# A two-layer trunk on one core: scan inputs on row quarters of TensorE, the angle products on ScalarE, the copies of q between the sines, three products of zeros at the begin in place of five

## The reference

```python
for l in range(DEPTH):                       # 2 layers
    h = rms_norm(x, norm1_g[l])
    u, q, k, v, g_ssm, g_attn = jnp.split(h @ w_in[l], splits, axis=-1)
    y_ssm = s5_branch(u, ...)                # below
    q = apply_rope(rms_norm(q, q_norm_g[l]), cos, sin)
    k = apply_rope(rms_norm(k, k_norm_g[l]), cos, sin)
    y_attn = moba_attention(q, k, v) @ w_attn[l]     # causal, one block of 256
    x = x + (sigmoid(g_ssm) * y_ssm + sigmoid(g_attn) * y_attn) @ w_out[l]
    x = x + hier_moe(rms_norm(x, norm2_g[l]), ...)   # 2 of 32 experts of width 512

# s5_branch: abar = exp(lam * dt) is complex, per group and state
bu = einsum('bsgh,gph->bsgp', u, bbar)       # re and im
s[t] = abar * s[t-1] + bu[t]                 # the scan over 256 tokens
y = re(einsum('bsgp,ghp->bsgh', s, c)) + d_skip * u
z = gelu(y);  val, gate = split(z @ w_glu);  return val * sigmoid(gate)
```

## Time and profile before

| | us |
|---|---|
| median of 3 runs | 1342.66 (1339.72 to 1344.41) |
| the profiled execution, its time | 1342.33 |
| its span, first to last instruction | 1340.4 |
| TensorE products busy | 1166.9 (87% of the span) |
| VectorE / ScalarE / GpSimd busy | 427.3 / 179.9 / 170.8 |
| DMA, mean over the span | 345 GB/s |
| mean granted clock of TensorE | 0.935 |

### The profile page before, as it was taken

How to read it: one execution, slowest core, us unless ns; L and a number is a source line. 1 busy time by engine, 2 the same in 40 slices (tenths; PEclk the granted TensorE clock), 3 DMA queues, 4 the chain that set the end, 5 groups by cost and what they waited for, 6 DMA issues and landing times.

```text
span 1340.4 us, 18306 instructions
## 1 busy us (share of the span) xinstructions
PE 1166.9 (87%) x7416; PEld 520.6 (39%) x7417; DVE 427.3 (32%) x863; ACT 179.9 (13%) x375; POOL 170.8 (13%) x186
## 2 busy tenths in 40 slices
PE   9999999999866887787799999999988876877677
PEld 6445546433321332233264455464333322332232
DVE  5789742411100110011087987232111101110011
ACT  1412412200000000000025124040000000000000
POOL 1757400000000000000035672000000000000000
PEclk9999999999988887898899999999998879888888
DMA  7533566999999999999973236869999999999997
GB/s 264 187 126 126 209 277 272 374 426 425 428 428 426 429 429 428 427 429 427 408 236 131 120 127 252 353 258 379 428 427 426 429 429 428 427 429 429 429 422 292
DMA packets 66520, 462.32 MB, mean 345 GB/s; under 512 B 20792, under 2 KB 21024, under 8 KB 40352
## 3 DMA queue, kind: packets, MB, share of 16 engines
q1 hardware_dynamic: 65680, 461.44, 83.4%
q10 hardware_dynamic: 784, 0.09, 0.0%
HBM read 460.47 MB, written 1.05 MB: 344 GB/s over the span
## 4 chain that ended last, share of the span: by engine, by line
PE 50%; DMA 38%; DVE 5%; SPq 4%; issue 2%; ACT 1%; DVEq 0%; ACTq 0%
DMA pool_all<-in_w_gate_up_dram 34%; PE ps L1077 16%; PE ps L825 8%; PE ps L859 4%; PE ps L1091 3%; SPq L522 3%; PE ps L884 3%; DMA pool_all<-in_w_down_dram 3%; PE ps L709 2%; PE ps L840 2%; PE ps L1036 2%; PE ps L728 1%; PE ps L743 1%; PE ps L1013 1%; PE ps L893 1%
## 5 line engine op out<-in xcount | busy, mean ns | idle before, releaser
L1077 PE MATMUL ps<-pool_all,xs 128*32 128x512 f32 (+1 forms) x2816 | 370.5, 687 | 134.7 <-DMA pool_all<-in_w_gate_up_dram 122.5
L1077 PEld LDWEIGHTS ps<-pool_all,xs 128*32 128x32 f32 x2816 | 97.8, 124 | 401.4 <-issue 400.2
L1869 DVE SCALAR_TENSOR_TENSOR rope<-rope,ps 128x512 f32<-128x512 f32 x22 | 15.1, 688 | 520.8 <-ACT rope L1412 520.8
L1091 PE MATMUL ps<-pool_all 128*32 128x512 f32 (+1 forms) x1408 | 159.3, 605 | 20.3 <-DMA pool_all<-in_w_down_dram 14.1
L825 PE MATMUL ps<-pool_all,hT 128*128 128x512 f32 x256 | 114.3, 598 | 0.0
L1412 ACT ACTIVATE rope<-ps 128x512 f32<-128x512 f32 x22 | 13.1, 597 | 640.6 <-PE ps L1077 640.6
L1091 PEld LDWEIGHTS ps<-pool_all 128*32 128x32 f32 x1408 | 46.0, 111 | 119.1 <-issue 117.7
L2134 POOL TENSOR_TENSOR pool_all<-pool_all 128x512 f32<-128x512 f32 x64 | 79.5, 1275 | 26.7 <-DVE pool_all L1647 21.2
L1036 PE MATMUL ps<-xs,pool_all 128*128 128x512 f32 x176 | 81.4, 605 | 0.0
L1013 PEld LDWEIGHTS ps<-pool_all,hT 128*128 128x128 f32 x640 | 73.0, 192 | 16.8 <-issue 16.8
L1013 PE MATMUL ps<-pool_all,hT 128*128 128x128 f32 x640 | 76.8, 278 | 0.0
(11 more groups left out here) (261 smaller groups left out, 1031.7 us busy)
## 6 DMA issues: line engine op xcount, KB each, us to landing
pool_all<-in_w_gate_up_dram SPq DMA_DIRECT2D x108, 2048.0 KB, 29.0
pool_all<-in_w_down_dram SPq DMA_DIRECT2D x58, 2048.0 KB, 26.8
pool_all<-in_w_in_dram SPq DMA_DIRECT2D x14, 2048.0 KB, 13.0
pool_all<-in_w_gate_up_dram SPq DMA_DIRECT2D x22, 1024.0 KB, 15.8
pool_all<-in_w_gate_up_dram SPq DMA_DIRECT2D x30, 512.0 KB, 7.4
pool_all<-in_w_glu_dram SPq DMA_DIRECT2D x4, 2048.0 KB, 11.1
pool_all<-in_w_out_dram SPq DMA_DIRECT2D x4, 2048.0 KB, 11.9
pool_all<-in_w_down_dram SPq DMA_DIRECT2D x6, 1024.0 KB, 19.1
```

Of the source, the lines that this page charges most:

```text
L1077: mm = pe.matmul(ps[r, half], xT[:, k // 4, k % 4, r], lane_cols(n, TRIO * h, k % 4, half), start=(k == 0), stop=(k == KC - 1), skip_group ...
L1091: mm = pe.matmul(ps[r, 2 + half], ffT[:, c, r], lane_cols(n, 2 * TRIO, c, half), start=(c == 0), stop=(c == 3), skip_group_check=True)
```

## The change

Five edits. (1) `scan_input` uses products of 32 rows (row quarters) in place of 64: the four tiles of a quad take the four quarters of the rows and write one bank each, 4 to 7; steps with even k use the left half of each bank, odd k the right half. Before, step k used only two banks, and halves of the rows. (2) Since all steps now share the four banks, step k >= 1 waits for `taken` (VectorE has done its four multiplications of step k - 1) in place of `scanned` (its scans of step k - 2), step 0 waits for `v_raw` (ScalarE has copied v), and the first glu product waits for the last scan. (3) ScalarE makes the products of step number and turns, 32 copies with a scale, of 129 columns, per layer; the low part goes to `sinT`, where the sines come later. (4) ScalarE's `heads_out(0)` stands between the sines of the first and of the second half. (5) `WARM` is 3.

```diff
-WARM = 5
+WARM = 3
+    taken = signal("taken", 8)
...
                 if k == 0:
                     pe.wait_ge(b_ready, at(b_ready, l, 4))
-                if k == 1:
                     pe.wait_ge(v_raw, at(v_raw, l, 2))
-                if k >= 2:
-                    pe.wait_ge(scanned, at(scanned, l, k - 1))
+                if k >= 1:
+                    pe.wait_ge(taken, at(taken, l, k))
                 for part in range(2):
-                    for j in (0, 2, 1, 3):
-                        r = slice(64 * (j // 2), 64 * (j // 2) + 64)
-                        mm = pe.matmul(ps[:, 4 + 2 * (k % 2) + j // 2, (2 * part + j % 2) * P:(2 * part + j % 2 + 1) * P],
+                    for j in range(4):
+                        r = slice(32 * j, 32 * j + 32)
+                        c = SEQ * (k % 2) + P * part
+                        mm = pe.matmul(ps[:, 4 + j, c:c + P],
                                        b_lhs[r, part, j % 2, q], uT[r, q, half * HALF:(half + 1) * HALF],
                                        start=True, stop=True)
...
                     if u == 0:
-                        pe.wait_ge(scanned, at(scanned, l, 7))
+                        pe.wait_ge(scanned, at(scanned, l, 8))
...
+        def setup_steps(h):
+            for turns, dst in ((turns_hi, turn_a[:, h]), (turns_lo, sinT[:, 8 * h:8 * h + 8])):
+                for i in range(8):
+                    act.activation(dst[:, i], const("step"), ACT.Copy, scale=turns[:, 8 * h + i:8 * h + i + 1]).then_inc(stepped, 1)
...
             setup_one(l)
-            for h in range(2):
-                setup_sines(l, h)
+            setup_steps(0)
+            setup_steps(1)
+            setup_sines(l, 0)
...
             heads_out(0)
+            setup_sines(l, 1)
             heads_std(0)
...
-            ve.tensor_tensor(a, step, wide(turns_hi[:, tiles], 2, [8, TW]), ALU.mult).then_inc(dve_layer, 1)
-            ve.wait_ge(dve_layer, S.next())
+            ve.wait_ge(stepped, at(stepped, l, TILES * (h + 1)))
             ve.tensor_scalar(b, a, ROUND, ROUND, ALU.add, ALU.subtract).then_inc(dve_layer, 1)
             ve.wait_ge(dve_layer, S.next())
             ve.tensor_tensor(a, a, b, ALU.subtract).then_inc(dve_layer, 1)
             ve.wait_ge(dve_layer, S.next())
-            ve.tensor_tensor(b, step, wide(turns_lo[:, tiles], 2, [8, TW]), ALU.mult).then_inc(dve_layer, 1)
-            ve.wait_ge(dve_layer, S.next())
-            ve.tensor_tensor(a, a, b, ALU.add).then_inc(dve_layer, 1)
+            ve.tensor_tensor(a, a, sinT[:, tiles], ALU.add).then_inc(dve_layer, 1)
...
-                for o, x, table in ((0, re, cs), (1, im, sn), (2, im, cs), (3, re, sn)):
-                    ve.tensor_tensor(out4[o], x, table, ALU.mult).then_inc(dve_layer, 1)
+                for o, x, table in ((0, re, cs), (1, im, sn), (2, im, cs)):
+                    ve.tensor_tensor(pre[:, o], x, table, ALU.mult).then_inc(dve_layer, 1)
                     L.add()
+                ve.tensor_tensor(pre[:, 3], re, sn, ALU.mult).then_inc(taken, 1)
```

More of the change, by code:

```diff
@@ L373, in trunk @@
     turn_ready, one_ready, turns_ready, tables_ready = signal("turn_ready"), signal("one_ready", 2), signal("turns_ready", 2), signal("tables_ready")
-    sin_ready, half_ready = signal("sin_ready", 2), signal("half_ready", 2)
+    stepped, half_ready = signal("stepped_or_sine", 2 * TILES + 2), signal("half_ready", 2)
     f_ready, expanded = signal("f_ready"), signal("expanded", 4)
@@ L384, in trunk @@
     first_rows, first_xT = signal("first_rows"), signal("first_xT")
-    dve_layer, dve_list = signal("dve_layer", 197), signal("dve_list", 25)
+    dve_layer, dve_list = signal("dve_layer", 185), signal("dve_list", 25)
     settled = signal("settled")
@@ L1230, in setup_sines @@
             act.activation(turn_b[:, h], turn_b[:, h], ACT.Square).then_inc(half_ready, 1)
-            act.activation(sinT[:, 8 * h:8 * h + 8], turn_a[:, h], ACT.Sin, scale=TWO_PI).then_inc(sin_ready, 1)
+            act.activation(sinT[:, 8 * h:8 * h + 8], turn_a[:, h], ACT.Sin, scale=TWO_PI).then_inc(stepped, 1)
         A = Counted(0, 0)
@@ L1461, in norm_turned, with angles @@
                                  ALU.mult).then_inc(hT_ready, 1)
-        def angles(S, h):
+        def angles(S, l, h):
             a, b = turn_a[:, h], turn_b[:, h]
             tiles = slice(8 * h, 8 * h + 8)
-            step = wide(const("step"), 1, [8, TW])
-            ve.tensor_tensor(a, step, wide(turns_hi[:, tiles], 2, [8, TW]), ALU.mult).then_inc(dve_layer, 1)
-            ve.wait_ge(dve_layer, S.next())
+            ve.wait_ge(stepped, at(stepped, l, TILES * (h + 1)))
             ve.tensor_scalar(b, a, ROUND, ROUND, ALU.add, ALU.subtract).then_inc(dve_layer, 1)
@@ L1582, in setup_second @@
                     ins.then_inc(tables_ready, 1)
-                    ve.wait_ge(sin_ready, at(sin_ready, n, 2))
+                    ve.wait_ge(stepped, at(stepped, n, 2 * TILES + 2))
                     ve.wait_ge(tables_ready, at(tables_ready, n, 1))
@@ L1603, in _ @@
                              ALU.mult).then_inc(uT_ready, 1)
-            angles(L, 0)
-            angles(L, 1)
+            angles(L, l, 0)
+            angles(L, l, 1)
             setup_second(l, L)
@@ L1622, in scan @@
                 tiles = slice(4 * q, 4 * q + 4)
-                b = 4 + 2 * (k % 2)
                 ve.wait_ge(bu_done, at(bu_done, l, k + 1))
-                cs, sn = (x[:, tiles, 0:HALF].rearrange("p (b j) t -> p b j t", b=2) for x in (cosT, sinT))
-                re, im = (ps[:, b:b + 2, r * SEQ:(r + 1) * SEQ].rearrange("p b (j t) -> p b j t", j=2) for r in range(2))
-                out4 = [pre[:, v].rearrange("p (b j) t -> p b j t", b=2) for v in range(4)]
+                cs, sn = (x[:, tiles, 0:HALF] for x in (cosT, sinT))
+                re, im = (ps[:, 4:8, SEQ * (k % 2) + P * r:SEQ * (k % 2) + P * r + P] for r in range(2))
                 if k > 0:
                     ve.wait_ge(scanned, at(scanned, l, k))
-                for o, x, table in ((0, re, cs), (1, im, sn), (2, im, cs), (3, re, sn)):
-                    ve.tensor_tensor(out4[o], x, table, ALU.mult).then_inc(dve_layer, 1)
+                for o, x, table in ((0, re, cs), (1, im, sn), (2, im, cs)):
+                    ve.tensor_tensor(pre[:, o], x, table, ALU.mult).then_inc(dve_layer, 1)
                     L.add()
-                ve.wait_ge(dve_layer, L.value() - 2)
+                ve.tensor_tensor(pre[:, 3], re, sn, ALU.mult).then_inc(taken, 1)
+                ve.wait_ge(dve_layer, L.value() - 1)
                 ve.tensor_tensor(pre[:, 0], pre[:, 0], pre[:, 1], ALU.add).then_inc(dve_layer, 1)
-                ve.wait_ge(dve_layer, L.next() - 1)
+                L.add()
+                ve.wait_ge(dve_layer, L.value() - 1)
+                ve.wait_ge(taken, at(taken, l, k + 1))
                 ve.tensor_tensor(pre[:, 2], pre[:, 2], pre[:, 3], ALU.subtract).then_inc(dve_layer, 1)
```

## The result

| | before | changed |
|---|---|---|
| median (range, runs), us | 1341.91 (1339.72 to 1344.41, 4) | 1331.74 (1330.0 to 1332.89, 4) |
| profiled execution, its span | 1342.33, 1340.4 | 1332.89, 1331.1 |
| TensorE / VectorE / ScalarE / GpSimd busy | 1166.9 / 427.3 / 179.9 / 170.8 | 1158.7 / 413.7 / 199.0 / 165.5 |

The ratio is 0.9928, with an interval of 0.991 to 0.9947: 9.7 us faster. A second set of runs gave 0.9931 (0.9917 to 0.9945; 1331.75 against 1340.8, 6 and 11 runs). The forecast was 1332.4.

A forecast was written before the change was run, and what follows sets the result against it. TensorE was taken to bound each layer's front, DMA the expert stage, so front savings move the end. 6.20 - 3.00 + 6.37 + 0.40 = 9.97 us off 1342.33 gives 1332.4 us, range 1329.5 to 1338.2.

The forecast's parts named there:

- The hole at L640: TensorE's idle time ahead of q's transposes goes: 4.97 us in layer 0, v's slowdown included, 1.23 in layer 1.
- The 1.70 us of v: First half of v behind the layer 0 hole returns to full clock: 7.03 us in place of 8.73.
- 37.9 us for the first sines: ScalarE's first sines in layer 0 start 3.7 us earlier than 41.61, as VectorE loses two angle products there.
- The wait ahead of the scan: First scan block now waits for ScalarE's v copies: costs 1.5 us in each layer, 3.0 in all.
- Row quarters: Scan blocks take 0.64 us, 0.455 less each; seven blocks per layer count, 14 in all, 6.4 us.
- block 7's gain: The last scan block's saving in each layer is not passed on: TensorE would arrive earlier and wait for VectorE.
- (a): Rival: row quarters in scan blocks are no faster than halves; sum 3.6 us, 1338.8 us; chance 0.10.
- (c): Rival: scan block passes on row quarters run one after another, 2.0 us per block, 1351.5 us; chance 0.04.
- Three zeros: Fewer zero products at TensorE's start: u starts 0.4 us earlier, limited by its weights' landing; the rest becomes idle time.
- (b): Rival: clock falls at new holes ahead of u and first scan blocks; two or three falls give 1335.8 to 1337.5; chance 0.10.
- (d): Rival: front's gain is not passed on, the experts' weight stream being the limit already; 1340 to 1342 us; chance 0.04.
- (e): Rival: hole at L640 stays because another condition, GpSimd's expanded matrices, is late; 1338.6 us; chance 0.02.

The follow-up runs named there:

- steps-only: The kernel before with only the angle products moved to ScalarE, q's copies still behind both sines: 1334.84 us, one run.
- copies-only: The kernel before with only ScalarE's copies of q put between the sines, angle products still on VectorE: 1336.46 us, one run.
- fillers: Changed kernel with earlier v copies, output-matrix transposes behind v, and two unused products ahead of u: 0.9898, 1327.61 us; again 0.9903, 1328.98 us.

## Why the prediction was right

**The hole at L640, 6.2 us.** Right. It is gone in both layers, 3.43 and 1.39 us. The 1.70 us of v came too (1.70 in layer 0 between the two profiled executions: 17.31 to 17.09, with the new hole of 1.5 inside), but the ground I gave for it holds only in part: of three executions with the hole of 3.19 to 3.27 us the clock fell in two. What I took for a cost of the hole is one that some executions have; that the profiled kernel before was one of them is luck. The estimate of 37.9 us for the first sines was met with the steps alone (37.60); in the changed kernel they came at 40.27, since VectorE began with its angles at 32.73, not at 30.91, and the angles then took 7.54 us for the forecast 7.0. Two operations of 16 columns had taken 1.04 and 0.98 us ahead of them, where they took 0.18 and 0.17 (the last section has the reason). It cost nothing, as either edit would do alone: the steps-only and the copies-only kernels show that step as it was argued.

**The wait ahead of the scan, -3.0 us.** Right: 1.45 us of idle time in each layer, released by ScalarE's copies of v, 15.58 to 17.09 us in length (1.51).

**Row quarters, 6.37 us.** Right in mechanism, 0.18 us small: 3.27 and 3.28 us for 3.19 twice. Seven blocks save 9.17 - 8.73 = 0.44 us each, not 0.455; the eighth passes on 0.23, and not nothing. (TensorE reaches the glu product 9.83 us after scan block 7 starts, 133.65 to 143.48, against 10.06. The block takes 0.66 us for 0.99, and the products on 64 rows behind it, L783, take 1.09 for 0.99.) The step that did not hold is that all of block 7's gain would be lost to waits for VectorE. No idle time stands ahead of the glu product: scan 7 ended at 140.19 + 3.19 = 143.38 us, just ahead of its start at 143.48. The glu product had 0.33 us of room behind scan 7 before and has 0.10 now. Nor does any idle time stand ahead of L791, at 150.45. The normalisation that I thought it wants ends 0.43 us behind its start before and 0.45 now, so these transposes never waited for all of it. `taken` is met in every step. Rivals (a) and (c) are excluded by the block of 0.65 us: a block on quarters takes half the rounds of one on halves, also with four banks written. The Trainium skill, page "TensorEngine Tiling (Array Packing)", section Theoretical Speedup, gives up to 4 times for 32 rows or less, from which the prediction had worked out 0.455 us for the block. The trace agrees for the passes alone, four rounds of 0.112 or 0.45 us; the block takes 0.2 us more.

**Three zeros, 0.4 us.** Not to be seen. In the profiled execution u began 0.18 us earlier, and the clock fell at the idle time ahead of u, for 1.66 us. This is the one fall that the forecast's range allowed for, and not rival (b), which needs two or three; at the two holes ahead of the scan there was none. In the second profile of the changed kernel the clock did not fall, and u began 0.21 us earlier. By itself the edit brings nothing that 10 runs can tell. This is the term that failed, by 0.4 us of 10. With three zeros u starts about 0.1 us behind the landing of its weights, which took 8.7 to 9.4 us from their issue in these executions. With five it starts 0.82 us behind the last of the transposes, when VectorE has copied them, at 10.84 to 11.80, as the clock rises early or late in the zeros. The 0.4 us is smaller than either scatter.

**The sum.** Forecast 9.97 us against 9.44 in the profiled execution. Terms of layer 0: 4.97 became 5.13 (3.43 + 1.70), 1.5 stayed at 1.5, 3.19 became 3.27, 0.4 became 0.18 - 1.66. Layer 1: 2.92 became 3.19. Some 0.8 came from stages that the change doesn't touch. That this hit 1332.4 so closely is partly luck: from the glu product of layer 0 to q's of layer 1 alone the executions of the table take 541.24 to 542.77 us, the u of layer 0 lost 1.66, and the fall behind the old hole was there to be won. Rivals (d) and (e) are out: both layers pass their gain to the stages behind.

## What to carry to other kernels

Two edits against one wait are judged apart: each alone removed this hole, so the second was worth nothing, and it showed only in kernels that had one of them. A wait that an edit adds at one place for the sake of fifteen others is worth a look of its own: a signal half a stage earlier, and independent work moved behind it, gave back 1.45 of its 1.51 us in each layer. Where a part is worth 0.3% or less, lengths between rows of two traces, which agree to 0.01 us here, tell it apart, and times from different sets of runs do not. A profile is one execution: here it was once the fastest of ten and four times the slowest of four, in the changed kernel too, so a length is taken from it, and the whole time is not.

## What the runs showed of the hardware

**The clock at the begin and ahead of u differs from execution to execution.** The passes of zeros, the first thing TensorE does, start 0.85 us apart (3.44 and 4.30 us in the changed kernel) and later 0.43 us apart (4.82 and 5.25), so at half the clock and then at the full one, 1.2 and 2.4 GHz; a window of the profile says 1.00 for all of it. The change from one to the other came at 4.5 us in this execution and at 7.1 in its second profile. That makes six passes last 4.26 or 5.49 us, and the idle time ahead of u 2.83 or 2.12. Of the five executions with three zeros and no fillers, the clock fell again ahead of u in the four in which it had risen at 4.5 to 5.2 us, behind 2.83, 2.74, 2.71 and 2.19 us of idle time (u's product then took 15.74 us; 0.81 in the window of 11 to 20 us). It stayed at 1.00 in the one in which it had risen at 7.1 us, behind 2.12. The idle times of 2.19 and 2.12 are too close to be the reason by themselves; in these five an early rise goes with the fall, and whether it is the reason was not tried. With fillers or five zeros the idle time was 0.51 to 1.06 us and there was no fall in any (14.05 to 14.08 us).

**The clock behind the hole at L640.** After a busy stretch of 40 us, a hole of 3.2 us had a fall behind it in two executions of three. 1.45 us ahead of the scan block and 0.97 to 1.34 us ahead of L640 had none in any.

**Row groups of 32.** Eight float32 products of 32 by 128 by 128 take 0.65 us, 16 passes in four rounds of 0.112 us and 0.2 around them; on halves of 64 rows it was 1.09 us, in eight rounds. The order of the products hardly matters (0.68 us when neighbours share a quarter).

**Small operations on VectorE beside GpSimd.** Two rows of GpSimd, in the changed kernel and in the kernel before:

```profile
29.11 2.08 POOL L2093 TENSOR_TENSOR pool_all<-pool_all,cst 128x512 f32<-128x512 f32 x2 [28.69 <-DMA qk_gain<-in_k_norm_g_dram]
```

```profile
29.87 2.07 POOL L2088 TENSOR_TENSOR pool_all<-pool_all,cst 128x512 f32<-128x512 f32 x2 [29.44 <-DMA qk_gain<-in_k_norm_g_dram]
```

VectorE's two 16-column operations of about 1 us (29.16 and 30.24) lie beside the first pair, one beside each product of 1.06 us. In the kernel before VectorE's last such operation had ended at 29.39, ahead of GpSimd. The other traces settle it. In both layers of all 14 profiled executions, each 16-column operation that began more than 0.01 us behind the start of one of these two products took 0.85 to 1.07 us, 35 in all, and ended 0.03 us behind the end of that product. None of those in the 3 us ahead of these products took over 0.18 us. GpSimd's products took 1.05 to 1.10 us with such an operation beside them, and 1.06 in layer 0 of the kernel before, where there was none. So it is VectorE's small operation that is held up until GpSimd's is done, and not the other way round.
